# Shorter steps for experts of at most 32 tokens, and the first step placed ahead of the second half of the gather

## The reference, cut to what matters

```python
logits = h @ w_router                      # [256, 8]
top_val, top_idx = top_k(logits, 2)        # two experts for each token
gate = softmax(top_val)
# for each expert e, over the tokens assigned to it:
#   y = (silu(x @ w_gate[e]) * (x @ w_up[e])) @ w_down[e]      widths 1024 -> 3584 -> 1024
# out[token] += gate * y
```

## Time and profile before

| | |
|---|---|
| median of 3 runs | 1672.86 us (1670.66 to 1673.17) |
| the profiled execution, its own time | 1672.14 us |
| its span | 1670.4 us |
| PE busy | 1544.0 us (92%) |
| DVE, ACT busy | 418.1 us (25%), 250.2 us (15%) |
| DMA, q1 | 483.70 MB, 75.8% of the span of 16 engines |
| in_w_exp_gate, _up issues | x128 each, 896.0 KB, 9.2 and 13.0 us to landing |

### The profile page before, as it was taken

One profiled execution on the slowest core, in us unless ns is written; L12 is line 12 of the kernel. 1 busy time (PEld: TensorE's weight loads), 2 busy tenths in 40 slices (PEclk: granted clock), 3 DMA queues, 4 the chain that ended last, 5 costly groups with the idle time before them and its releaser, 6 DMA issues.

```text
span 1670.4 us, 21757 instructions
## 1 busy us (share of the span) xinstructions
PE 1544.0 (92%) x8696; PEld 852.4 (51%) x8697; DVE 418.1 (25%) x955; ACT 250.2 (15%) x560; POOL 0.2 (0%) x4
## 2 busy tenths in 40 slices
PE   5988889999989998599999999999999999999996
PEld 2777658777657774444444443443333443333332
DVE  2366525333344533600002000110000300003003
ACT  2132210000012331110101010011111111111112
POOL 0000000000000000000000000000000000000000
PEclk8999799999999998799999999999999999999998
DMA  9974525765656440068979797999999999997991
GB/s 348 380 266 164 189 101 192 273 252 202 227 193 229 172 178 16 1 264 332 407 289 407 284 408 294 408 374 405 408 407 407 407 377 407 407 408 296 367 377 78
DMA packets 168185, 484.43 MB, mean 290 GB/s; under 512 B 10024, under 2 KB 20544, under 8 KB 168000
## 3 DMA queue, kind: packets, MB, share of 16 engines
q1 hardware_dynamic: 168128, 483.70, 75.8%
HBM read 482.63 MB, written 1.05 MB: 290 GB/s over the span
## 4 chain that ended last, share of the span: by engine, by line
PE 79%; DMA 9%; DVE 5%; SPq 3%; ACT 2%; issue 2%; DVEq 0%; ACTq 0%
PE bank L1024 11%; PE bank L931 9%; PE bank L1064 8%; DMA ring<-in_w_exp_up 8%; PE bank L778 7%; PE bank L1008 6%; PE bank L1185 6%; PE bank L1020 5%; PE bank L949 4%; PE bank L912 4%; PE bank L1058 3%; PE bank L1211 3%; PE bank L772 3%; SPq L629 2%; PE bank L1280 2%
## 5 line engine op out<-in xcount | busy, mean ns | idle before, releaser
L1024 PE MATMUL bank<-ring,hT 128*64 128x448 f32 x1280 | 255.1, 546 | 32.2 <-DMA ring<-in_w_exp_up 12.7
L1024 PEld LDWEIGHTS bank<-ring,hT 128*64 128x64 f32 x1280 | 89.0, 137 | 190.7 <-issue 153.7
L931 PE MATMUL bank<-hT,ring 128*128 128x256 f32 x704 | 158.0, 385 | 1.7 <-DVE hT L1429 1.7
L778 PE MATMUL bank<-hT,ring 128*128 128x256 f32 x640 | 153.0, 396 | 3.9 <-ACT hT L1953 2.5
L1809 DVE TENSOR_TENSOR bt<-arena,bank 64x512 f32<-64x512 f32 (+2 forms) x36 | 24.3, 675 | 493.5 <-PE bank L1024 249.6
L931 PEld LDWEIGHTS bank<-hT,ring 128*128 128x128 f32 x704 | 135.2, 193 | 24.1 <-issue 3.8
L778 PEld LDWEIGHTS bank<-hT,ring 128*128 128x128 f32 x640 | 124.5, 198 | 26.0 <-DVE hT L1429 4.4
L1064 PE MATMUL bank<-ring,bt 128*32 128x256 f32 (+1 forms) x1232 | 136.8, 445 | 0.0
L1348 DVE SCALAR_TENSOR_TENSOR acc<-ring,cond,acc 128x512 f32<-128x512 f32 x140 | 105.2, 752 | 4.9
L1020 PE MATMUL bank<-ring,hT 128*128 128x448 f32 x256 | 100.7, 546 | 4.1 <-DMA ring<-in_w_exp_up 3.4
L1008 PE MATMUL bank<-ring,hT 128*32 128x448 f32 x1024 | 102.8, 542 | 0.0
(11 more groups left out here) (279 smaller groups left out, 1179.8 us busy)
## 6 DMA issues: line engine op xcount, KB each, us to landing
ring<-in_w_exp_gate SPq DMA_DIRECT2D x128, 896.0 KB, 9.2
ring<-in_w_exp_up SPq DMA_DIRECT2D x128, 896.0 KB, 13.0
ring<-in_w_exp_down SPq DMA_DIRECT2D x64, 1536.0 KB, 15.9
ring<-in_w_ada SPq DMA_DIRECT2D x24, 2048.0 KB, 9.4
ring<-in_w_in SPq DMA_DIRECT2D x10, 2048.0 KB, 12.8
ring<-in_w_exp_down SPq DMA_DIRECT2D x32, 512.0 KB, 16.3
ring<-in_w_ff_gate SPq DMA_DIRECT2D x5, 2048.0 KB, 12.4
ring<-in_w_ff_up SPq DMA_DIRECT2D x5, 2048.0 KB, 12.8
```

Of the source, the lines that this page charges most:

```text
L778: last = mm(o[:, 0:T], w[:, k, t * P:(t + 1) * P], hT[:, k, :], start=(k == 0), stop=(k == KC - 1))
L931: last = mm(bank[n % 2][:, a * T:(a + 1) * T], w[a][:, k, t * P:(t + 1) * P], hT[:, k, :], start=(k == 0), stop=(k == KC - 1))
L1024: last = mm(o[64 * c2:64 * c2 + 64, 64 * c2:64 * c2 + EH], xsT[:, k, t0:t0 + 64], w[:, k, c2 * EH:(c2 + 1) * EH], start=(k == 0), stop=(k ...
```

## The change

1. A new class 0, for at most `TINY = 32` tokens (`route[:, 1]`, which the other path of the kernel uses, is raised to at least 1). With the token counts above, experts 0, 5 and 7 get it; expert 1 (54 tokens) keeps class 1.
2. A class-0 expert is worked with `tiny_step`: `quarter` for gate and up, one unit's transposes, a down pass of four matmuls of 256 columns beside each other.
3. `STREAM_AT` puts the last in rank (expert 7) at position 2, in the first stage, expert 1 at position 4 and expert 5 at position 6.
4. Job 0 runs between the two halves of the gather; the second half goes to banks 4, 5, 6, 1. VectorE's and ScalarE's orders follow. `has_small` tells the loop that job 0 is done.
5. The loop on each of TensorE, VectorE and ScalarE reads two more values in each iteration (`has_small`, and the class at position `2 * ends`), and has one more body in each place where a small step can stand.

```diff
-STREAM_AT = (0, 1, 3, 5, 7, 2, 4, 6)
+STREAM_AT = (0, 1, 3, 5, 7, 4, 6, 2)
+HAS_SMALL = [int(l_ != LONE and (l_, s_) != (0, 0)) for l_ in range(4) for s_ in range(ES)]
+SECOND_BANKS = (4, 5, 6, 1)
+TINY = 32
-UNITS = {1: [("half", 0)], ...
+UNITS = {0: [("quarter", 0)], 1: [("half", 0)], ...
...
+        def has_small(eng, l, i):
+            return eng.value_load(plan_i[0:1, bass.ds(ES * l + i + 36, 1)], min_val=0, max_val=1)
...
-            for h in range(2):
+            def gather(h, banks):
                 pe.wait_ge(sel_v, 2 + h)
...
+            gather(0, range(4))
...
+            def tiny_step(J, ends):
+                if ends is not None:
+                    pe.wait_ge(xsS_v, ends + 1)
+                    pe.wait_ge(yacc_v, 4 * ends + 12)
+                for k in range(0, KC, 2):
+                    pe.wait_ge(full_g[k // 2], 16 * J + 16)
+                    pe.wait_ge(full_u[k // 2], 16 * J + 16)
+                    quarter(TX, range(k, k + 2), True)
+                pe.wait_ge(yzS_v, 1 if ends is None else ends + 1)
+                pe.wait_ge(eh_v, 4 * J + 4)
+                h, one_ = hs[64:P, 0, :], ident[64:P, 64:P]
+                mm(bank[3][:, 0:64], h[:, 0:P], one_, start=True, stop=True)
+                for t in range(1, 4):
+                    last = nc.tensor.transpose(bank[3][:, t * 64:(t + 1) * 64], h[:, t * P:(t + 1) * P], one_)
+                last.then_inc(et_p, 4)
+                down(J, 0, 0, ALL, (0,), 7)
...
             with pe.If(misfit == 0):
+                tiny = class_at(pe, 0)
                 pe.wait_ge(xsS_v, 1)
-                turn_scatter_weights(0, bank[3])
+                with pe.If(tiny == 0):
+                    tiny_step(0, None)
+                with pe.Else():
+                    small_step(0, None)
+                gather(1, SECOND_BANKS)
+                turn_scatter_weights(0, bank[0])
+                pe.wait_ge(sgt_a, 1)
                 with nc.Fori(0, 4, engines=PE, head_slot={PE[0]: 0}) as l:
                     which = class_at(pe, 2 * l + 1)
                     with pe.Fori(0, ES) as i:
                         J = job_ahead(pe, l, i)
                         ends = ends_seen(pe, l, i)
-                        with pe.If(l != LONE):
-                            small_step(J, ends)
+                        partner = has_small(pe, l, i)
+                        tiny = class_at(pe, 2 * ends)
+                        with pe.If(partner == 1):
+                            with pe.If(tiny == 0):
+                                tiny_step(J, ends)
+                            with pe.Else():
+                                small_step(J, ends)
...
                         with pe.If(l == 0):
-                            small_step(J + 2, ends)
+                            with pe.If(tiny == 0):
+                                tiny_step(J + 2, ends)
+                            with pe.Else():
+                                small_step(J + 2, ends)
...
# VectorE: the ranking
-            then(ts(total, sums, float(CAPS[0]), 1.0, ALU.is_gt, ALU.add))
-            for cap in CAPS[1:]:
+            then(ts(total, sums, float(TINY), None, ALU.is_gt))
+            for cap in CAPS:
                 then(stt(total, sums, float(cap), total, ALU.is_gt, ALU.add))
...
+            then(ts(route[:, 1, 0:NE], route[:, 1, 0:NE], 1.0, None, ALU.max))
...
# VectorE: stream_end (ScalarE's alike, with c in (0, 1))
-                nc.vector.tensor_copy(ys[64:P, 1, CW:D], bank[7][64:P, :]).then_inc(ys_v, 1)
+                with ve.If(class_at(ve, 2 * g) == 0):
+                    for c in (2, 3):
+                        last = nc.vector.tensor_copy(ys[64:96, 1, c * T:(c + 1) * T], bank[7][32 * c:32 * c + 32, 0:T])
+                    last.then_inc(ys_v, 1)
+                with ve.Else():
+                    nc.vector.tensor_copy(ys[64:P, 1, CW:D], bank[7][64:P, :]).then_inc(ys_v, 1)
...
# VectorE: the way in
-                stream_weights(0)
                 gathered(0)
                 small_window(None)
+                nc.vector.memset(bank[7][:, :], 0.0).then_inc(yzS_v, 1)
+                with ve.If(tiny == 0):
+                    stream_step(0, 0)
+                with ve.Else():
+                    stream_step(0, 1)
+                stream_weights(0)
                 gathered(1)
                 large_window(1)
-                ve.wait_ge(sgt_p, 1)
-                stream_weights(1)
                 signal(nc.vector.memset(ys, 0.0), dv)
                 nc.vector.tensor_copy(yacc, xs[:, :, :]).then_inc(yacc_v, 4 * NE + 1 - 20)
                 for i in (4, 5, 6):
                     last = nc.vector.memset(bank[i][:, :], 0.0)
                 last.then_inc(yzL_v, 1)
-                ve.wait_ge(sgt_a, 1)
-                nc.vector.memset(bank[7][:, :], 0.0).then_inc(yzS_v, 1)
+                ve.wait_ge(sgt_p, 1)
+                stream_weights(1)
```

More of the change, by code:

```diff
@@ L72 @@
 C_PLAN = C_IOTA + NE
-NPLAN = 40
+NPLAN = 52
 C_END = C_PLAN + NPLAN
@@ L271 @@
 CAPS = (64, 96, 160)
-UNITS = {1: [("half", 0)], 2: [("half", 0), ("quarter", 64)], 3: [("wide", 0), ("quarter", 128)],
+TINY = 32
+UNITS = {0: [("quarter", 0)], 1: [("half", 0)], 2: [("half", 0), ("quarter", 64)], 3: [("wide", 0), ("quarter", 128)],
          4: [("wide", 0), ("wide", 128)]}
@@ L1002, in hidden, with quarter @@
                         last.then_inc((eg_p, eu_p)[a], 3 if n == 1 else before_last(n, i))
-            def quarter(t0, ks):
+            def quarter(t0, ks, alone=False):
                 for k in ks:
@@ L1011, in quarter @@
                             last.then_inc(u_used if q == 3 else g_used, 1)
+                        elif alone and k == KC - 2 and q % 2:
+                            last.then_inc(eu_p if q == 3 else eg_p, 3)
             def stream_hidden(J, n, i, a, t0, c=0):
@@ L1177, in up_parts @@
                 for part_, (lo, hi) in enumerate(((0, SPLIT), (SPLIT, EH))):
-                    if part_:
+                    if part_ and ends is not None:
                         pe.wait_ge(yacc_v, 4 * ends + 12)
@@ L1306, in _ @@
             with pe.Else():
+                gather(1, range(4, 8))
                 with nc.Fori(0, NE, engines=PE, head_slot={PE[0]: 0}) as r:
@@ L1806, in stream_step @@
                     up_ready(J, n, i)
[L1807 removed]
+                    rows_, o = (slice(64, P), bank[2]) if n != 1 and i == ITEMS[n] - 1 else (slice(0, P), bank[1])
                     n_ = EH if n == 3 and i < 2 else CW
@@ L1875, in _ @@
                         J = job_ahead(ve, l, i)
-                        with ve.If(l != LONE):
-                            stream_step(J, 1)
+                        partner = has_small(ve, l, i)
+                        tiny = class_at(ve, 2 * ends_seen(ve, l, i))
+                        with ve.If(partner == 1):
+                            with ve.If(tiny == 0):
+                                stream_step(J, 0)
+                            with ve.Else():
+                                stream_step(J, 1)
                         with ve.If(which == 3):
@@ L1882, in _ @@
                         with ve.If(l == 0):
-                            stream_step(J + 2, 1)
+                            with ve.If(tiny == 0):
+                                stream_step(J + 2, 0)
+                            with ve.Else():
+                                stream_step(J + 2, 1)
                             with ve.If(i == 1):
@@ L2034, in _, with gathered @@
             act(gt[:, :, 1], gt[:, :, 0], ACT.Exp).then_inc(r_a, 1)
-            for h in range(2):
+            def gathered(h, banks):
                 for g in (1, 3):
@@ L2161, in stream_end @@
                         large_out(2, jobs)
-                act(ys[64:P, 1, 0:CW], bank[7][0:64, :], ACT.Copy).then_inc(ys_a, 1)
+                with ae.If(class_at(ae, 2 * g) == 0):
+                    for c in (0, 1):
+                        ins = act(ys[64:96, 1, c * T:(c + 1) * T], bank[7][32 * c:32 * c + 32, 0:T], ACT.Copy)
+                    ins.then_inc(ys_a, 1)
+                with ae.Else():
+                    act(ys[64:P, 1, 0:CW], bank[7][0:64, :], ACT.Copy).then_inc(ys_a, 1)
                 scatter_weights_in(g + 1, bank[7])
@@ L2167, in _ @@
             with ae.If(misfit == 0):
-                scatter_weights_in(0, bank[3])
+                tiny = class_at(ae, 0)
+                with ae.If(tiny == 0):
+                    stream_step(0, 0)
+                with ae.Else():
+                    stream_step(0, 1)
+                gathered(1, SECOND_BANKS)
+                scatter_weights_in(0, bank[0])
                 with ae.Fori(0, 4) as l:
@@ L2172, in _ @@
                         J = job_ahead(ae, l, i)
-                        with ae.If(l != LONE):
-                            stream_step(J, 1)
+                        partner = has_small(ae, l, i)
+                        tiny = class_at(ae, 2 * ends_seen(ae, l, i))
+                        with ae.If(partner == 1):
```

(5 more changed lines are left out.)

18 lines of the change are left out of this document (11 added, 7 removed).

## The result

The changed kernel takes 1931.5 us (1931.0 to 1934.4 in 4 runs) against 1672.1: a ratio of 1.1556, interval 1.1536 to 1.1576. It is 259 us slower; I had forecast 5 us faster and a range that ended at 1678. Its profiled execution took 1934.4 us, its span is 1932.5.

What follows compares the result with a forecast made beforehand. Transfers and the large step's buffer order bound the first stages, TensorE the last. 1487.3 + 172.3 + 4.7 + 0.8 = 1665.1 us of span, 1666.8 with 1.7 around it, median 0.7 above: 1667.5 us, range 1661 to 1678.

Steps and rivals of the forecast that it cites:

- A rule against the change: TensorE's loop: some 2050 instructions after, from 1456 recorded, against room for 2048; taken branches outside the window wait for fetches.
- rival C: Last stage: code no longer stays, 3.17 us at entry and three boundaries, 12.7 us in all, so 1680.2; chance 0.15.
- The first stage's period: First stage: transfers and the large step's order set 92.61 us a period, against 92.98 measured; only 0.4 to give.
- The lags behind the scatters: After the first and second stages' scatters: short steps make up TensorE's lag, 3.7 us and 3.2 us.
- The way in: Before the loop: job 0 between gather halves starts job 1 at 725.0, job 2's gate issue 3.1 us earlier.
- 18.24 + 1.67: Job 1's first passes: today's time plus 1.67 us for the low clock, which job 1 pays instead of job 0.
- the pause of 3.8 us ahead of job 0: Ahead of job 0: after the change TensorE's pause is short enough that job 0 pays no low clock.
- The tiny step: Each of 12 small steps: 12.4 us against 19.84, 89 us of TensorE time, nearly all hidden by transfers or buffer order.
- The reads: Last stage: two added register reads an iteration, 1.56 us at each of three boundaries, 4.7 us slower.

Runs made afterwards that it cites:

- flat kernel: The changed kernel with TensorE's loop alone rewritten so the small, tiny and large bodies stand once each, 1568 instructions: 1674.4 us, ratio 1.0021.
- the move alone: The kernel before with job 0, in the small form, put between the halves of the gather; no tiny form, no added reads: 1676.2 us, ratio 1.0033.
- reordered kernel: flat_in_loop with VectorE's list on the way in reordered, yacc written and bank 7 cleared ahead of the other clears: 1656.3 us, ratio 0.9913.
- 96 dead matmuls: The kernel before with a never-run body of 96 matmuls in TensorE's loop, 1993 instructions: 1925.0 us, ratio 1.153.
- `reads`: The kernel before with two more register reads in each inner iteration of TensorE, VectorE and ScalarE: 1680.1 us, ratio 1.0051.
- flat_in_loop: The flat kernel with both gather halves first, job 0 in the loop in tiny form, two reads an iteration: 1663.9 us, ratio 0.9963.

## Why the prediction was wrong

**The step that failed** is *A rule against the change* with rival C's price. I had the count: 1456 recorded instructions, and some 2050 with the tiny bodies. I gave the rival 0.15, and 12.7 us. It came with 259 us, and its 12.7 would already have lain outside of my range. The Trainium skill, "Runtime: NRT & Kernel Launch", section "Instruction fetch mechanics", gives TensorE room for 2048 instructions. By that rule's figure the runs agree roughly: the edge lies between 1865 and 1993 counted instructions, waits not counted. Three things in my pricing were wrong:
- *The unit.* I took the one cold gap of 3.17 us for the price of a jump. The queue shows one packet of instructions in it (before, 778.6 to 781.9: `q8 instruction: 1, 0.02, 2.1%`), so it is one packet's price (3.4 us in the gap of the last stage, 4.3 in that of the second), and a boundary of the last stage took seven of them, 23.8 us. What one cold jump costs in a kernel whose code stays says nothing on how many fetches an iteration makes when it doesn't.
- *The place.* I held it to the last stage and let transfers hide the rest. But 183 of the 262 us came ahead of the last stage: a gap of 17 us behind each large step is longer than the slack of a pair (54.1 us of transfers against 19.84 + 30.2 of TensorE's two steps), and with one buffer for the weights a TensorE that stands stops the transfers as well.
- *The argument against.* "The path itself is short, and may stay after its first pass" is refuted: all three boundaries of the last stage pay the full price (23.81, 23.74 and 24.29 us), though only one body runs in it.

**The first stage's period**, 92.61 us, was right with the code in its room: 92.4 and 92.5 in the flat kernel (841.23, 933.61, 1026.15).

**The lags behind the scatters** were right: job 10 to job 15 146.4 us in the flat kernel (146.7 predicted), job 19 to job 23 108.9 (108.2), against 150.4 and 111.4.

**The way in** was wrong by sign. 3.1 us earlier was the forecast for job 4; counted from the gather it is 4.4 later with the move alone and 9.8 in the flat kernel. In the changed kernel the path from the first window copy (691.82) to job 1's start (728.33) took 36.5 us, against my 28.9. Its chain:

```profile
692.55 7.92 PE bank L1017 x62
700.54 1.28 ACT L2118
...
704.71 6.12 PE bank L1075 x56
...
724.61 3.72 issue
728.33 21.36 PE bank L1031 x48
```

`quarter` takes 7.92 instead of 6.20 and the down pass 6.12 instead of 3.34: the clock is 0.65 from 692.50 to 696.00, behind the pause at the gather's end, and 0.51 from 704.70 to 710.80, after TensorE had waited for the silu, its table load (1.28, as foreseen) and the copies. Then 3.72 at the loop's entry, where I had 0.5; how much of it is the five reads and how much a fetch, no run tells apart. These three terms, 1.7 + 2.8 + 3.2, are the 7.6 us. Behind them come 21.36 for three passes where 18.24 + 1.67 was the term. That the pause of 3.8 us ahead of job 0 would cost nothing came from one row and didn't hold.

**The tiny step** (12.4 us) holds where the clock stays: `quarter` 6.22 in the reordered kernel, and in the changed kernel's chain 2.88 from the end of `quarter` to the down pass (817.90 to 820.78) and 3.23 for that pass. **The reads** were 0.70 for 0.78; their follow-up at the clock was missing.

So with its code in its room the change's parts are: the tiny form about 14 us of gain in the reordered frame (14.3 was the sum for its effect through both scatters and job 0: 3.7, 3.2 and 7.4), the way in 5.5 of loss, the reads up to 8.5 of loss, the positions nothing that shows. The parts are from different frames, and don't add up to the flat kernel's 3.5 of loss: -14 + 5.5 and half of the reads' 8.5 are -4. What the changed kernel itself would be with the room and each of its parts undone in turn was not run.

## What to carry to other kernels

Before adding a body to a loop whose steps are unrolled, count the instructions of the whole loop, those of the bodies that don't run included, and look at the packets of the instruction queue in the page: they must not grow with the iterations. Here two added bodies cost 259 us, one of them taken out gave 242 back, and the same work with each body once cost none of it. When two profiles are compared by absolute times, compare first where the part ahead of the change ends: here, for the same work, it ended between 678.8 and 684.7 us. A shorter step is worth something only where TensorE, not the transfers or the order in which buffers come free, ends the wait; and a pause of two microseconds can cost as much again in clock.

## What the runs showed of the hardware

- TensorE's loop of 1606 counted instructions (before) runs its last stage, 142 us, with two packets of 16 KB on the instruction queue. At 1865 and 1874 executions of one kernel lie 20 and 35 us apart. From 1993 on its code is fetched in each iteration: nine packets in an iteration, in the changed kernel and in that with 96 dead matmuls, 161 to 170 in the execution for 32, and 256 to 281 us more in kernels that execute the work of before.
- A packet of instructions that TensorE stands for takes 3.2 us (one in the gap of 3.17, before) to 4.3 us (four in 17.11, changed kernel).
- A register read costs TensorE 0.70 us where nothing covers it (`reads`; 0.77 between the gaps of flat and flat_in_loop).
- In `reads` the granted clock was 0.65 in the 4 us behind a pause of 2.15 us in which no matmul ran, 0.59 behind one of 2.12 us, and 1.00 behind one of 2.11 us.
